# PSUM banks awaited at the matmul that first writes them, and the constants at the first transposes

## The reference

```
for l in range(2):                                   # first block
    h = hybrid_mixer(x, ...)      # x @ w_in, two attentions, a gated mixture,
                                  # three branches gated and merged, @ w_mix_out
    x = layer_norm(ALPHA * x + h, ln1)
    h = memory_cross_attention(x, mem, wq, wkv, wo)
    x = layer_norm(ALPHA * x + h, ln2)
    h = conv_ffn(x, w_up, conv_k, conv_b, w_down)    # x @ w_up, conv, gelu(a) * b, @ w_down
    x = layer_norm(ALPHA * x + h, ln3)
# second block, one layer
xn = rmsnorm(x)                                      # xn @ w_in_2, a recurrence, a sparse attention
merged = sigmoid(g_a) * (y_a @ proj_a) + sigmoid(g_b) * (y_b @ proj_b)
h = x + merged @ w_out
return h + square(relu(rmsnorm(h) @ w_mlp_in)) @ w_mlp_out
```

## Time and profile before

| what | value |
|---|---|
| median of 3 runs | 1701.44 us (1701.34 to 1701.44) |
| the profiled execution's own time | 1697.92 us |
| its span, first to last instruction | 1695.1 us |
| PE busy | 1566.9 us, 92% of the span |
| VectorE busy | 1028.1 us, 61% |
| ScalarE busy | 801.3 us, 47% |
| GpSimd busy | 240.1 us, 14% |
| mean clock granted to PE | 0.961 |

### The profile page before, as it was taken

One profiled execution on the slowest core, in us unless ns is written; L12 is line 12 of the kernel. 1 busy time (PEld: TensorE's weight loads), 2 busy tenths in 40 slices (PEclk: granted clock), 3 DMA queues, 4 the chain that ended last, 5 costly groups with the idle time before them and its releaser, 6 DMA issues.

```text
span 1695.1 us, 25368 instructions
## 1 busy us (share of the span) xinstructions
PE 1566.9 (92%) x10403; PEld 1411.2 (83%) x10403; DVE 1028.1 (61%) x1704; ACT 801.3 (47%) x1435; POOL 240.1 (14%) x225
## 2 busy tenths in 40 slices
PE   7969989989998999998989999799988799989999
PEld 5859988889986789987779988587976699879887
DVE  3735477578765576467478764446664486646733
ACT  3525444456643445544446652353445564435532
POOL 1300032031101230032131110103010041100000
PEclk8979999999999999999999999799999899999999
DMA  7682254345555534244445555455211244635453
GB/s 268 244 149 100 88 187 174 103 171 180 193 203 174 174 125 139 87 155 174 144 149 178 192 175 177 140 181 207 98 54 47 75 141 147 204 106 193 158 191 124
DMA packets 41027, 261.33 MB, mean 154 GB/s; under 512 B 4512, under 2 KB 5152, under 8 KB 14672
## 3 DMA queue, kind: packets, MB, share of 16 engines
q1 hardware_dynamic: 35600, 238.44, 41.0%
q0 software_dynamic: 2944, 15.69, 3.8%
q10 hardware_dynamic: 2368, 5.58, 0.9%
HBM read 254.98 MB, written 4.19 MB: 153 GB/s over the span
## 4 chain that ended last, share of the span: by engine, by line
PE 66%; DVE 15%; ACT 8%; issue 4%; DMA 4%; POOL 3%; ACTq 0%; POOLq 0%; DVEq 0%; SPq 0%
PE ps L471 59%; DVE lows L1485 5%; ACT wh L984 3%; PE ps L567 3%; DMA d_scr<-PT 2%; POOL sm L2170 2%; PE ps L653 1%; ACT S L1397 1%; DVE ar L1988 1%; DVE sm L1518 1%; DVE xs L1515 1%; DMA raw<-d_wst 1%; PE ps L674 1%; ACT arR L1466 1%; DVE S L2050 1%
## 5 line engine op out<-in xcount | busy, mean ns | idle before, releaser
L1485 DVE TENSOR_TENSOR lows<-raw,wh 128x1024 fp32r<-128x1024 f32 (+3 forms) x473 | 545.1, 1171 | 274.1 <-ACT wh L984 271.1
L471 PE MATMUL ps<-xTr,wh 128*128 128x256 f32 (+2 forms) x3664 | 674.0, 286 | 10.7 <-DVE xTr L1504 6.3
L471 PEld LDWEIGHTS ps<-xTr,wh 128*128 128x128 f32 (+2 forms) x3664 | 575.0, 193 | 15.4 <-issue 7.3
L984 ACT CAST wh<-raw 128x1024 fp32r<-128x1024 f32 (+3 forms) x473 | 455.9, 989 | 177.3 <-DMA raw<-d_wst 149.5
L471 PE MATMUL ps<-xTr,lows 128*128 128x256 f32 (+2 forms) x1832 | 522.0, 285 | 0.0
L471 PEld LDWEIGHTS ps<-xTr,lows 128*128 128x128 f32 (+2 forms) x1832 | 352.4, 192 | 0.0
L471 PE MATMUL ps<-wh,arR 128*128 128x512 f32 x928 | 298.6, 401 | 16.8 <-DVE ar L1638 4.6
L471 PEld LDWEIGHTS ps<-wh,arR 128*128 128x128 f32 x928 | 177.3, 191 | 60.4 <-DVE ar L1638 9.3
L471 PE MATMUL ps<-lows,arR 128*128 128x512 f32 x464 | 185.6, 400 | 0.0
L471 PE MATMUL ps<-arR,wh 128*128 128x256 f32 (+1 forms) x832 | 148.2, 281 | 2.2 <-DVE lows L1485 2.2
L471 PE MATMUL ps<-wh,xTr 128*128 128x512 f32 x384 | 127.3, 412 | 19.1 <-DMA cst<-d_cst 9.7
(11 more groups left out here) (265 smaller groups left out, 1546.4 us busy)
## 6 DMA issues: line engine op xcount, KB each, us to landing
raw<-d_wst SPq DMA_DIRECT2D x196, 1024.0 KB, 4.8
raw<-d_wst SPq DMA_DIRECT2D x24, 512.0 KB, 3.5
raw<-d_wst SPq DMA_DIRECT2D x12, 896.0 KB, 4.6
raw<-d_wst SPq DMA_DIRECT2D x8, 672.0 KB, 4.7
ar<-d_lnp POOLq DMA_DIRECT2D x5, 1024.0 KB, 5.1
raw<-d_wst SPq DMA_DIRECT2D x8, 441.0 KB, 3.4
d_scr<-PT POOLq DMA_DIRECT2D x1, 3072.0 KB, 35.3
ar<-d_par POOLq DMA_DIRECT2D x2, 1192.0 KB, 9.6
```

Of the source, the lines that this page charges most:

```text
L471: op = e.matmul(out, s, m, start=start and i == 0, stop=stop and i == len(pairs) - 1)
L984: e.copy(high_of(m), raw_of(m)).then_inc(*high.done(m))
L1485: e.tensor_tensor(low_of(m), raw_of(m), high_of(m).bitcast(F32), ALU.subtract).then_inc(*low.done(m))
```

## The change

The wait moves out of the reservation. `reserve` fixes the order of banks and the readers, without a wait. `ready` issues the wait, and it is called ahead of each run of matmuls, so the wait stands ahead of the first that writes that bank; later calls give a wait that was already passed. `take` does both at once as before, for `features` and the banks of `A`. The wait for the constants moves from ahead of the first product to ahead of the first transposes.

```
 class Banks:
     def rewind(self):
-        self.i, self.until = -1, [None] * len(self.banks)
+        self.i, self.until, self.before = -1, [()] * len(self.banks), {}
+
+    def reserve(self, name, *until):
+        self.i = (self.i + 1) % len(self.banks)
+        self.before[name], self.until[self.i] = self.until[self.i], until
+        self.place[name] = self.i
+
+    def ready(self, w, name):
+        if self.before[name]:
+            w.wait_ge(*self.before[name])
+        return self[name]
 
     def take(self, w, name, *until):
-        self.i = (self.i + 1) % len(self.banks)
-        if self.until[self.i]:
-            w.wait_ge(*self.until[self.i])
-        self.until[self.i] = until
-        self.place[name] = self.i
-        return self.banks[self.i]
+        self.reserve(name, *until)
+        return self.ready(w, name)
...
# tokens, and tokens_by_tile alike
-                bk = [M.take(w, (*name, i), *until, i) for i in range(2)]
+                for i in range(2):
+                    M.reserve((*name, i), *until, i)
...
-                        run(bk[i][:, :], pairs, a == 0, a == 6).then_inc(*product.done(*name, i))
+                        b = M.ready(w, (*name, i))
+                        run(b[:, :], pairs, a == 0, a == 6).then_inc(*product.done(*name, i))
...
# down
-                acc = [[M.take(w, (*name, i, h), vec, "res", *name, i, h) for h in range(2)] for i in range(2)]
+                for i in range(2):
+                    for h in range(2):
+                        M.reserve((*name, i, h), vec, "res", *name, i, h)
...
-                        run(acc[i][h][:, :], three(Y.h[:, k, c], Y.l[:, k, c], wH[:, 0, f], wL[:, 0, f]),
+                        b = M.ready(w, (*name, i, h))
+                        run(b[:, :], three(Y.h[:, k, c], Y.l[:, k, c], wH[:, 0, f], wL[:, 0, f]),
                             k == 0, k == kt - 1).then_inc(*product.done(*name, i, h))
...
# start of the PE program
                 e.matmul(b[:, :], osb[:, 0:128], osb[:, 0:512], start=True, stop=True)
-            w.wait_ge(cst_in)
...
                 tokens(("v", l), W, span(CV, 512), X, [], (act, "v", l))
+                w.wait_ge(cst_in)
                 qk_turned(0, 0)
```

## The result

The changed kernel takes 1669.78 us (median of 4 runs, 1668.23 to 1670.89); the kernel before, run beside it, takes 1701.39 us (4 runs). The ratio is 0.9818 [0.9801, 0.9835], or 28 to 34 us less. The profiled execution took 1670.89 us with a span of 1669.1 us; that of before took 1697.92 us with 1695.1. So the two profiles differ by 26.0 us in span and 27.0 us in time, and the medians by 31.6 us.

A forecast was written before the change was run, and what follows sets the result against it. The prediction took TensorE (PE), 66% of the span, as the bound, standing still in waits for constants and PSUM banks. Gains of 25.4 us gave 1672.5 from the profiled 1697.92, plus 3.5 made 1676.0 us; range 1671 to 1685.

The forecast's parts named there:

- I carry that over: Whole kernel: the run median's 3.5 us above the profiled execution was added to 1672.5, giving 1676.0.
- the sum, 25.4: Whole kernel: all forecast gains added, 25.4 us, with low ends adding to 19.5 and high ends to 27.1.
- The start, 9.8: First products: removing the constants wait gains 9.8 us with the clock up, 8.2 if the first 12 matmuls run slow.
- `mix_out`, 2.8 twice: Both `mix_out` products: matmuls start before the last banks are free; 2.8 us each, between 2.1 and 3.5.
- `dn`, 1.6 and 3.3: The `dn` products: the 1.9 us gap closes, gaining 1.6 us in the first layer and 3.3 in the second.
- the short wait for the third piece: In `dn`, after its gap closes: the third weight piece is late; first-layer subtraction ends at 484.87, PE wants it at 484.6.
- `out` and `fin`, 5.1: `out` gains 1.6 us as its gap closes; `fin` gains 3.5, or 2.1 if slow.
- The clock keeps its slow stretches: Rival, all changed places: PE stops and starts elsewhere, every term has its low end, 1681.9 us; chance 0.16.
- Transfers collide: Rival, at the start: earlier weight loads compete with other transfers, PE loses 2.6 us at worst, 1678.6; chance 0.09.
- The bias write swallows the start: Rival, first attention: the write stays put, its 13.3 us wait grows by 9.8, time 1685.8; chance 0.08.
- nothing happens: Rival, bank waits: other waits on the same counters keep the gaps, time 1701.4; chance 0.03.
- slower: Rival, `tokens` products: early restart leaves the clock low; with all 192 matmuls slow, 1716 us; chance 0.02.

The follow-up runs named there:

- the 47: Executions of the unchanged kernel before, on two chips, with spans of 1694.0 to 1702.8 us; the medians on the two chips are 1700.13 and 1700.41 us.
- filling the gaps: Kernel before with 11 more warm-up products and unread dummy products ahead of each `down` product that has a gap, waits unmoved: 1688.72 us against 1700.41, ratio 0.9925.
- `tokens` experiment: Kernel before with `reserve` and `ready` only in `tokens` and `tokens_by_tile`, `down` unchanged: 1698.59 us against 1700.41, ratio 0.9992; its profile has a span of 1700.5.

## Why the prediction was right and wrong

**The failed step: "The median of the runs is 1701.44, 3.5 above it; I carry that over."** That treats the distance of the profiled execution from the median as a constant of the kernel, and no reason is given for it. It is not one. That the profiled execution of before was one of the shortest is chance (4 of 47 are as short); the median span of the 47 is 3.0 us longer (1698.1 against 1695.1), and the spans go with PE's clock; in the changed kernel the median is 1.1 us below the profiled execution. The miss of 1676.0 - 1669.78 = 6.2 us is made of 3.5 (carried over), 1.1 (the profiled execution after is above its median), 1.0 (2.8 us outside the span before, 1.8 after, in all four runs; why it is less stays open) and 0.6 (the sum, 25.4 against 26.0). That the sum came so close is luck in part: `wo` lost 1.54 us by chance, and without it the stages gained 27.5 us, 2.1 more than forecast.

How much of the 3.0 us lay behind the gaps that the change removes, and so had to be counted as gain, is shown for one execution only. In the long one above, the first `dn` and the two `mix_out` lose 1.7 + 1.4 + 1.2 = 4.3 us more than in the profile of before. Its span is 31.4 us above that of the profile after, whose `wo` is slow as well, and 27.5 + 4.3 = 31.8 accounts for that. For the median execution it stays open. For it speaks that the spans of the four kernels with the bank waits moved scatter less about their means (standard deviation 1.2 us, 16 runs) than those of the kernel before (2.1 us, 47 runs). Against it speaks that in the two other profiles of before the seven changed places lose 8.4 and 9.0 us, about as much as the 8.7 in the first, and that filling the gaps did not shrink the spread (2.4 us, 6 runs).

**The start, 9.8.** Right in size and course: 10.06. The clock was taken as up because the granted clock read 1.00 at 12 to 13. The conclusion held, the evidence did not: without any warm-up the column reads 1.00 there as well, while the matmuls are 0.43 us apart (last section). The 0.23 us between matmuls after the change and the comparison without warm-up are what show it.

**`mix_out`, 2.8 twice.** The mechanism was right: six matmuls, three, three, with gaps of 0.38 and 1.37 us (0.8 and 1.7 forecast). I took the middle between a kept clock (3.5) and a lost one (2.1); it was kept in both layers, and the stages gained 3.55 and 3.79. At the place itself, in the first layer, the 13th matmul starts 243.16 - 238.23 = 4.93 us after the end of the last merge, against 256.76 - 248.03 = 8.73, which is 3.80. The rule of the Trainium skill (Perfetto Trace Analysis, Matmul Optimizations) that matmuls be issued back to back gave 2.1; the trace does not agree with it for gaps of this length, as the matmuls behind all four took 0.50 us. Behind the longer gaps ahead of `mix_out` before, 4.56 and 4.39 us with first matmuls of 0.77 us, it agrees.

**`dn`, 1.6 and 3.3.** The gaps closed as said, but the short wait for the third piece is not there. I had taken the subtraction at 483.70 for the third piece, and it is the fourth; the third was done earlier. So the 25th matmul starts 473.10 - 467.38 = 5.72 us after the start of the last `up` matmul, against 486.56 - 478.71 = 7.85: the first `dn` gained 2.1 us at the place, of which 1.39 is left at the next root; where the rest goes is not shown. The second gained 3.66. That the length of the first matmul tells the clock does not hold everywhere: the second `dn` of the `tokens` experiment starts with 0.47 us and then runs slow, with pairs of 1.06 us.

**`out` and `fin`, 5.1.** Right as a sum: 5.09. In `fin` the gap after nine matmuls is 0.24 us (0.3 forecast).

**The rivals.** *The clock keeps its slow stretches:* it did not; the first matmuls at all changed places take 0.40 to 0.50 us. *Transfers collide:* they do, but the one that loses is `x`, not the weights. GpSimd's first use of it stands in its timeline after the change as

```profile
10.26 0.74 POOL L2189 DMA_DIRECT2D xs<-d_x  x1
32.26 6.58 POOL L2195 TENSOR_SCALAR xs<-xs 128x1024 f32<-128x1024 f32 x2 [21.26 <-DMA xs<-d_x]
```

and at 25.80 before. With the constants alone moved it is 32.46, with the banks alone 25.75, so it is the earlier start that delays it. PE loses nothing by it: apart from the two waits at the start its waits for weight pieces are those of before, five of 5.0 us in all. The Trainium skill (Trainium Kernel Development and Optimization, Key Constraints) has transfers of different queues share the engines, and the trace agrees; the time that followed from it, 1678.6, did not come. *The bias write swallows the start, nothing happens, slower:* the write moved by 10.06 us and the wait behind it stayed 13.3, so none of them.

## What to carry to other kernels

Wait for a PSUM bank where it is first written, not where the product begins: here that alone was worth 19.2 us by medians and 16.4 between profiles, though each of the six gaps was only 1.6 to 4.6 us, because the matmuls behind a gap may run at half speed as well. A sum of terms made against one profiled execution belongs to that execution; before a distance to the median is carried over, ask whether it can be made of the very stretches that the change touches. A gap that leaves the clock up in the one trace at hand is no proof that it does so in most executions.

## What the runs showed of the hardware that was not expected

- The same gap at the same place leaves the clock at 2.4 GHz in one execution and at 1.2 in another: 1.89 us ahead of the first `dn` with a first matmul of 0.47 us before and 0.77 in the `tokens` experiment, and 2.00 us ahead of `wo` with pairs of 0.63 and 1.06 us. Counted over the five profiles in which `down` takes its banks ahead and the gaps are not filled (before three times, constants alone, `tokens` alone), the product ran slow behind 10 of 10 gaps of 4.3 to 4.6 us, 4 of 5 of 2.4, 6 of 10 of 1.9 and none of 5 of 1.6; behind the 2.00 us ahead of `wo`, over all ten profiles and both layers, in 8 of 20 cases. The gaps of 0.24 to 1.38 us in the changed kernel left it up in the profile.
- The granted clock reads 1.00 at the start also where the matmuls run at half speed. In the kernel without warm-up, whose matmuls come 0.43 us apart until 14.79, a window there holds four matmuls (six in the window from 483 of the kernel before, at 2.4 GHz) and says

```profile
12.00:13.00 1.00, 1.00 (x4) 0.80 (x3) 0.20 (x1) 0.00 (x0) 0.00 (x0) 1.00 1.05 434
```

- `x`, issued at 10.3 us in both kernels, is used from 25.80 before and from 32.26 after, 6.5 us later, while the weight loads that PE releases come sooner: SyncE issues eight of them in the first 36 us in place of six, and the windows from 22 to 28 us show 414 GB/s in place of 217.
